# The output projection goes group by group; eight modulation matrices become rows between the gates

## The reference, cut to what matters

```
m   = silu(cond) @ mod_w + mod_b                      # 6 x 1024 values: sh1, sc1, g1, sh2, sc2, g2
h   = rms(x) * gain * (1 + sc1) + sh1
y   = mixer(h)                                        # layer 0: recurrent block, layer 1: pooling
x   = x + g1 * (rms(y) * gain)                        # the post norm
h   = rms(x) * gain * (1 + sc2) + sh2                 # the pre norm of the feed-forward part
x   = x + g2 * (rms(swiglu(h)) * gain)
```

```
gate, rec = split(h @ w_in);  u = conv4(rec)
a = exp(-8 * sigmoid(u @ wa + ba) * softplus(-lam));  b = sqrt(1 - a^2) * sigmoid(u @ wx + bx) * u
hf, hb = scan forward, scan backward of (a, b)
y = ((hf + hb) * gelu(gate)) @ w_out
```

## Time and profile before

| | |
|---|---|
| three runs, us | 2396.31, 2398.34, 2401.71 (median 2398.34) |
| profiled execution, us | 2397.51, span 2395.5 |
| busy, us (share of the span) | PE 2252.5 (94%), DVE 1378.0 (58%), POOL 974.1 (41%), ACT 840.7 (35%) |
| mean granted TensorE clock | 0.967 |
| w_lo of a weight on POOL (line 2186), 157 | 4.7 us each |
| w_hi of a weight on ACT (line 1194), 157 | 1.9 us each |
| load of a modulation matrix to raw, 42 | 5.1 us to landing |
| x_old from the stored residual, 1.5 MB | 7.4 us to landing |

### The profile page before, as it was taken

The page is one execution under the profiler, slowest core; times in us unless marked ns, Lnnn a source line. Parts: engine busy times, 40 slices in busy tenths (PEclk is TensorE's granted clock), DMA queues, the critical chain, the costliest instruction groups (busy, mean ns, idle before and its releaser), DMA issues.

```text
span 2395.5 us, 31600 instructions
## 1 busy us (share of the span) xinstructions
PE 2252.5 (94%) x12840; PEld 2215.0 (92%) x12840; DVE 1378.0 (58%) x2356; ACT 840.7 (35%) x1143; POOL 974.1 (41%) x380
## 2 busy tenths in 40 slices
PE   7888899896999999999999999899999999999996
PEld 4887899886999999999999999899999999999995
DVE  7679977856665566432466468558363232442344
ACT  3477763024311111222343455544352122111232
POOL 3433313444202210444562676575465265222441
PEclk8999999898999999999999999999999999999997
DMA  8211125343223333344232454353234233321322
GB/s 277 98 63 55 56 68 188 117 149 115 88 95 101 105 124 101 110 141 133 87 134 97 131 178 131 106 184 124 97 132 141 71 120 129 104 88 53 104 86 92
DMA packets 209616, 274.01 MB, mean 114 GB/s; under 512 B 4744, under 2 KB 192704, under 8 KB 208960
## 3 DMA queue, kind: packets, MB, share of 16 engines
q1 hardware_dynamic: 180544, 221.47, 28.1%
q10 hardware_dynamic: 27200, 41.09, 5.0%
q0 software_dynamic: 1728, 9.44, 1.0%
HBM read 243.66 MB, written 28.32 MB: 114 GB/s over the span
## 4 chain that ended last, share of the span: by engine, by line
PE 66%; DVE 10%; ACT 2%; issue 2%; POOL 1%; DMA 1%; ACTq 0%; DVEq 0%; POOLq 0%
PE bank L819 63%; DVE y L1748 3%; DVE y L1735 1%; DVE pool_sum L2091 1%; DVE mod_sum_norms L1665 1%; PE bank L867 1%; PE bank L898 1%; POOL w_lo L2186 1%; DVE hid_lo L2002 1%; DVE wide L1798 1%; DVE mv_lo L1785 1%; PE bank L887 1%; DVE wide L2113 0%; DMA raw<-in_l_ffn_w_in 0%; DVE mv_lo L2149 0%
## 5 line engine op out<-in xcount | busy, mean ns | idle before, releaser
L2186 POOL TENSOR_TENSOR w_lo<-raw,w_hi 128x2048 fp32r<-128x2048 f32 x157 | 735.1, 4695 | 1178.2 <-ACT w_hi L1194 1178.0
L819 PE MATMUL bank<-mv_hi,w_hi 128*128 128x384 f32 (+2 forms) x2736 | 931.5, 340 | 27.2 <-DVE mv_lo L1869 9.3
L819 PE MATMUL bank<-mv_lo,w_hi 128*128 128x384 f32 (+2 forms) x2736 | 923.5, 338 | 0.0
L819 PE MATMUL bank<-mv_hi,w_lo 128*128 128x384 f32 (+2 forms) x2736 | 923.0, 337 | 0.0
L819 PEld LDWEIGHTS bank<-mv_hi,w_hi 128*128 128x128 f32 x2736 | 519.2, 190 | 31.8 <-issue 25.5
L819 PEld LDWEIGHTS bank<-mv_lo,w_hi 128*128 128x128 f32 x2736 | 519.5, 190 | 0.0
L819 PEld LDWEIGHTS bank<-mv_hi,w_lo 128*128 128x128 f32 x2736 | 518.9, 190 | 0.0
L1194 ACT ACTIVATE w_hi<-raw 128x2048 fp32r<-128x2048 f32 x157 | 295.8, 1908 | 528.3 <-DMA raw<-in_l_ffn_w_out 216.1
L819 PE MATMUL bank<-hid_hi,w_hi 128*128 128x384 f32 (+2 forms) x1056 | 362.5, 343 | 19.7 <-DVE hid_lo L2002 19.5
L2020 DVE TENSOR_TENSOR y<-y,bank 128x384 f32<-128x384 f32 (+2 forms) x480 | 262.2, 554 | 202.1 <-PE bank L819 202.1
L1999 DVE TENSOR_TENSOR hid<-hid,bank 128x384 f32<-128x384 f32 (+2 forms) x132 | 72.9, 553 | 516.1 <-PE bank L819 513.9
(11 more groups left out here) (138 smaller groups left out, 1773.7 us busy)
## 6 DMA issues: line engine op xcount, KB each, us to landing
raw<-in_l_ffn_w_in SPq DMA_DIRECT2D x92, 1024.0 KB, 5.1
raw<-in_l_ffn_w_out SPq DMA_DIRECT2D x46, 1024.0 KB, 4.9
raw<-in_l_mod_w SPq DMA_DIRECT2D x42, 1024.0 KB, 5.1
residual<-y ACTq DMA_DIRECT2D x10, 1536.0 KB, 7.2
x_old<-residual ACTq DMA_DIRECT2D x10, 1536.0 KB, 7.4
raw<-in_l_w_in SPq DMA_DIRECT2D x8, 1024.0 KB, 5.4
mod_stage<-in_l_mod_w SPq DMA_DIRECT2D x6, 1024.0 KB, 12.9
recurrence<-lru_f POOLq DMA_DIRECT2D x8, 576.0 KB, 3.1
```

The source lines that it names most:

```text
L819: last = pe.matmul(out, w, x, start=start and n == 0, stop=stop and n == len(steps) - 1)
L2186: pool.tensor_tensor(w_lo[:, slot(w), :], raw[:, q % 2, :], w_hi[:, slot(w), :].bitcast(F32), ALU.subtract).then_inc(w_ready, 1)
```

## The change

1. Matrices 6 and 7 become rows like 0 to 5, and so do 8 to 15: one of them in each stage of the gates, product behind the gate units, turn behind the fills. ACT copies the row into `raw` and adds the bias. Matrices 16 to 19 stay sums.
2. In the gates `u_split_lo` and the lo parts of six weights (granules 4 to 9) move from POOL to VectorE.
3. The output projection goes group by group over all 8 tiles. Three weights fit, so weights 0 and 1 are loaded and split a second time for groups 1 and 2. ACT takes the result from PSUM, once squared, once as it is. VectorE makes the lo parts of the mixed rows of groups 1 and 2 and three of the weights' lo parts.
4. The norms of the mixer and their pre norms are planned and run beside the products, as in the later steps. The first feed-forward block is done for groups 0 and 1, then for group 2, with the same weights. `ffn_first` goes.

```diff
-STEPS = [together(range(NB - TURN)) + snake(list(range(NB - TURN, NB))),
+STEPS = [[(0, (0, 1)), (0, (2,))] + together(range(1, NB - TURN)) + snake(list(range(NB - TURN, NB))),
+WOUT_LOADS = (0, 1, 2, 3, 0, 1)
+WOUT_TURNS = ((0, 1, 2, 3), (1, 2, 3, 4), (2, 3, 4, 5))
-    order += MIX_PHASES[:-1] + mods(0, 8, 10) + MIX_PHASES[-1:]
-    order += [("w_out", 0)] + mods(0, 10, 12) + [("w_out", 1)] + mods(0, 12, 14) + [("w_out", 2)]
-    order += mods(0, 14, 20) + [("w_out", 3)]
+    for item in MIX_PHASES:
+        order.append(item)
+        order += mods(0, *MODS_BEHIND.get(item, (0, 0)))
+    order += [("w_out", 0)] + mods(0, 17, 18) + [("w_out", 1), ("w_out", 2), ("w_out", 3)] + mods(0, 18, 20)
+    order += [("w_out", 4), ("w_out", 5)]
...
-            units += gate_units(n, j) + FILLS[n, j]
+            m = FIRST_MODS + 2 * n + j
+            units += gate_units(n, j) + [("row", m, 0, 0)] + FILLS[n, j] + [("turn", m, 0, 0)]
...
+                if kind == "row":
+                    row_product(bank[P_BANK[p]][0:2, 0:2 * P], n).then_inc(p_ready, 1)
+                    return
+                if kind == "turn":
+                    pe.wait_ge(p_freed, UNIT["row", n, 0, 0] + 1)
...
+            def out_projection(g, upto):
+                for i in range(KT):
+                    n, w = O_WOUT + KT * g + i, WEIGHT["w_out", WOUT_TURNS[g][i // 2]]
+                    upto(AT_WOUT[n - O_WOUT])
...
+            def take_wout(g, i):
+                n, m = O_WOUT + KT * g + i, wout_tile(g, i)
+                if i == 0:
+                    act.wait_ge(*((acc_ready[g - 1], 2) if g else (mixed_ready, KT)))
+                act.wait_ge(out_ready, n + 1)
+                src = bank[OUT_BANK[n]][:, 0:GT]
+                act.activation(norm_squares_of(g, 1)[:, m], src, ACT.Square).then_inc(squares[g], 1)
+                squared[g] += 1
+                act.activation(group(y, g)[:, m], src, ACT.Copy).then_inc(wout_taken, 1)
...
             for n in range(NLB):
                 for j in range(2):
                     s = 4 * n + 2 * j
                     lru_input(s)
                     lru_input(s + 1)
                     if n < NLB - 1:
                         conv(n + 1, j)
+                    for w in NEXT_GRANULES["gates", (2 * n + j - 1) // 2, 1 - j] if s else []:
+                        split_lo(w)
+                    if j == 1 and n < NLB - 1:
+                        u_split_lo(n + 1, 0)
                     lru_step(s)
+                    if j == 1 and n < NLB - 1:
+                        u_split_lo(n + 1, 1)
                     lru_step(s + 1)
...
+            def first_norms(g):
+                yield
+                norm_begin(g)
+                yield from post_norm(g, 0, 1)
+                yield
+                norm_begin(g)
+                yield from pre_norm_split(g, 0, 2, 24)
```

More of the change, by code:

```diff
@@ L304, in product_times @@
     at, t, one = {}, 0.0, (GT + 32) / 2400
+    for n in W_OUTS:
+        t += 3 * KT * one
+        at["out", n] = t
     for what, n in PRODUCTS:
@@ L316 @@
 AT_PRODUCT = {"gate": 3 * KT * (GT + 32) / 2400, "out": 3 * HB * (GT + 32) / 2400}
+AT_WOUT = [AT["out", n] - AT_PRODUCT["gate"] for n in W_OUTS]
 def merged(times, chains):
@@ L343, with places @@
 ENDLESS = 1e9
+FIRST_END = 200.0
+PLACES = range(0, KT, 2)
+def places(t):
+    return [t + k / KT * AT_PRODUCT["gate"] for k in PLACES]
 def out_time(layer, g, m=KT - 1):
@@ L364, in feed_forward_work @@
     work, hooks = [], []
+    for i, n in enumerate(W_OUTS):
+        hooks += places(AT_WOUT[i])
+        work.append(("ACT", ("take", n), AT["out", n], TAKE))
+    for w, t in J1_SPLITS.items():
+        low = ("DVE", 2.2) if w in DVE_SPLITS else ("POOL", SPLIT_LO)
+        work += [("ACT", ("split", w), t, SPLIT_HI), (low[0], ("split", w), t + SPLIT_HI, low[1])]
+    for g, t in ((1, MIXED_T[0]), (2, MIXED_T[1])):
+        for part, (t0, t1) in enumerate(MIXED_PARTS):
+            work += [("ACT", ("mixed", g, part), t + part * 1e-3, 0.45 * (t1 - t0)),
+                     ("DVE", ("mixed", g, part), t + 0.5 + part * 1e-3, 0.5 * (t1 - t0))]
     for layer in range(2):
-        for s in range(1 - layer, len(STEPS[layer])):
+        for s in range(len(STEPS[layer])):
             groups = STEPS[layer][s][1]
             t = AT["gate", PAIR[layer, s, groups[0], 0]] - AT_PRODUCT["gate"]
-            w = WEIGHT["down", layer, s]
-            work += [("ACT", ("split", w), t, SPLIT_HI), ("POOL", ("split", w), t + SPLIT_HI, SPLIT_LO)]
+            if own(layer, s) == s:
+                w = WEIGHT["down", layer, s]
+                t += DOWN_LATER if (layer, s) == (0, 0) else 0.0
+                work += [("ACT", ("split", w), t, SPLIT_HI), ("POOL", ("split", w), t + SPLIT_HI, SPLIT_LO)]
             for g in groups:
@@ L446, in post, with first_norm, first_residual, first_split @@
         return ends
+    folded = [put(("PE", "mods", 0), 0.0, FOLD) for _ in range(2)]
+    for m in range(FIRST_SUM + 2, 20):
+        t = put(("DVE", "mods", 0), 0.0, MOD_SUM)
+        folded.append(put(("PE", "mods", 0), t, FOLD))
+    scale = put(("DVE", "mods", 0), folded[-1], 2 * SMALL)
+    chain = "first"
+    spread, landed = {}, {}
+    def first_norm(g):
+        squared = [due["ACT", "take", O_WOUT + KT * g + i] + TAKE for i in range(KT)]
+        landed[g] = put(("ACT", chain, g), squared[-1], 0.1) + LANDING
+        spread[g] = norm(chain, g, squared)
+    def first_residual(g):
+        ends = post(chain, g, max(landed[g], spread[g]))
+        sq = squares(chain, g, ends)
+        put(("ACT", chain, g), ends[-1], 0.1)
+        spread[g] = max(scale, norm(chain, g, sq))
+    def first_split(g):
+        hi = []
+        for k in range(KT):
+            t = put(("DVE", chain, g), spread[g], FIRST_DVE)
+            hi.append(put(("ACT", chain, g), t, OP["ACT"]))
+            if k >= SPLIT_LAG - 1:
+                t = put(("DVE", chain, g), hi[k - SPLIT_LAG + 1], FIRST_DVE)
+        for k in range(KT - SPLIT_LAG + 1, KT):
+            t = put(("DVE", chain, g), hi[k], FIRST_DVE)
+        s = next(s for s, (b, groups) in enumerate(STEPS[0]) if g in groups)
+        assert t < AT["gate", PAIR[0, s, g, 0]], (g, t, AT["gate", PAIR[0, s, g, 0]])
+    first_norm(0)
+    first_residual(0)
+    first_split(0)
+    first_norm(1)
+    first_residual(1)
+    first_norm(2)
+    first_split(1)
+    first_residual(2)
+    first_split(2)
     for g in range(NG):
@@ L989, in _ @@
                 kind, n, j, g = u[0], u[1], u[2], u[-1]
-                if (kind, n) not in seen:
+                if (kind, n) not in seen and kind not in ("row", "turn"):
                     seen.add((kind, n))
@@ L2342, in after_pairs @@
         first = PAIR[layer, s, STEPS[layer][s][1][0], 0]
-        if first:
-            places |= {first + i + lag: MOD["mod", *m] for i, m in enumerate(mods)}
+        places |= {first + i + lag: MOD["mod", *m] for i, m in enumerate(mods)}
     return places
```

599 lines of the change are left out of this document (322 added, 277 removed).

## The result

The kernel after takes 2370.7 us (median of 4 runs, 2367.4 to 2374.5), the kernel before 2397.3 (median of 4, 2389.7 to 2401.7): 26.6 us less, ratio 0.9887, 95% interval 0.9869 to 0.9905. Forecast were 2345 and a gain of 53.5, range 2326 to 2370. The profiled execution took 2369.3 us, its span is 2367.5.

What follows compares the result with a forecast made beforehand. Taken as bounds: VectorE at the start, VectorE with POOL in its way in the gates, a chain of small steps in the output projection. 9.5 + 3 + 3.2 + 37.8 = 53.5 us less gave 2345 us, range 2326 to 2370.

Steps and rivals of the forecast that it cites:

- Start: Up to the first product: matrices 6 and 7 as rows bring it from 70.87 to near 61.5, minus 9.5 us.
- eight rows of 3.6 and eight turns behind each other from 21.1 end at 52: Start: TensorE's row products and turns run back to back, ending at 52 us where the last turn ended at 61.6.
- The tail of 9.3: Start: coefficient, affine, hi and lo after the last turn, 9.3 us before the first product, taken as unchanged.
- Gates: Lo parts to VectorE, eight rows to TensorE: TensorE needs 206 us plus 3.6 idle, 209.7 in all, minus 3.
- Its chain becomes 39.6 - 8.1 - 11.5 = 20 us shorter, 193 us: Gates: VectorE regains 39.6 us lost to POOL and takes on 8.1 of u_lo and 11.5 of weight splits.
- 193 / 8: Gates: VectorE's chain of 193 us spread evenly over eight stages, 24.1 us each.
- two stages with three fills at 29.0 us: Gates: a stage with three fills asks 29.0 us of TensorE, one with a single fill 20.6.
- The rival of the turn behind ScalarE's copy: Gates: turn waits for ACT's copy behind tanh, exp and sqrt; 225 us, 12.4 above before, total 2360; chance 0.13.
- plus 31: Gates: upper bound, all of today's idle and slow time stays beside the new row work; lower bound minus 7.
- Rest of the input projection: Four folds of 0.8 us go where TensorE is full: minus 3.2 us.
- Output projection: With first feed-forward step: floor 199.8 us plus 13 of norm waits, 212.8 instead of 250.57, minus 37.8.
- Behind it: After 664.6 us order and work stay: the same 1731 us, within 3.

Runs made afterwards that it cites:

- Experiment 4: Kernel after with half of the tiles left out of each of the first eight row products: 2363.5 us, first product at 59.02.
- Experiment 2: Kernel before with only the gates' lo parts (u and weights 4 to 9) moved from GpSimd to VectorE, no rows there: 2398.8 us, ratio 1.0005.
- 11: Kernel after with ScalarE copying the row before Exp and Sqrt, full rows, and ScalarE's two Sqrt a stage left out: 2356.5 us.
- 6: Kernel after with ScalarE copying the row before Exp and Sqrt, and seven of eight products of each row among the gates left out: 2370.7 us.
- 10: Kernel after with the row copied before Exp, an eighth of each gate row's products, and ScalarE's two Sqrt a stage left out: 2354.5 us.
- all six kernels with these gates: The kernel after and five follow-up kernels whose gates have the same instructions; their gates took 219.6 to 223.7 us, mean 221.5.
- 8: Kernel after with rows, copies and turns of matrices 14 and 15, the two in the last pair of stages, left out: 2362.3 us.
- 5: Kernel after with ScalarE copying each gate row right behind the two Tanh instead of behind Exp and Sqrt: 2369.0 us.
- Experiment 12: Kernel after with GpSimd taking the mixer's first-group lo parts ahead of the lo part of w_out's second weight: 2363.6 us.
- 13: Kernel after with the lo parts of the output projection's fifth and sixth weight on VectorE instead of GpSimd: 2358.9 us.
- Experiment 3: Kernel after with the gates' lo parts back on GpSimd, the eight rows kept: 2367.0 us, gates 221.6.
- experiment 17: Kernel after with mixer lo parts ahead of the weight's on GpSimd, and the output projection's last two weights' lo parts on VectorE: 2354.4 us, ratio 0.9826.

## Why the prediction was wrong

**Start, 5.1 us short.** The failed step is "eight rows of 3.6 and eight turns behind each other from 21.1 end at 52". It left out the six norm steps that stand between them in TensorE's queue (0.83 and 0.93 us each, 5.3 together) and began 1.9 us early. The tail of 9.3 that I kept was 8.2, which took 1.1 of the miss back. Experiment 4 shows that this chain, and not a landing, was the bound.

**Gates, 14 us short, half of the miss.** The terms that could be read from rows were right: 128x1152 at 1.36 us, the split at 2.29 (2.3 forecast), TensorE's work 206 (207.9 measured), low idle. Counted on TensorE in the profiled execution, the 14 us are 6.0 more idle time than the 3.6 forecast, 6.2 of lower clock, nearly all of it behind the two turns, which the sum put at nothing, and 1.9 of work. What failed is the step before: "Its chain becomes 39.6 - 8.1 - 11.5 = 20 us shorter, 193 us", "against a VectorE chain of 193 / 8 = 24.1". It took VectorE's busy time, freed of GpSimd, for the length of a stage. Experiment 2 gives VectorE that time alone and gains nothing. In the kernel after no pair's length is one engine's sum alone. In the first three pairs three limits lie within a few us: TensorE's work with the rows, 54.0 and 58.3 us in the first and third (11); with nearly all of the rows taken out, still 54.9, 56.8 and 59.2 (6); and with ScalarE's block shortened as well, 52.5, 54.4 and 56.2 (10). Shortening any one, by 18 us of rows, 10 of convolution or 21 of Sqrt in the three, gave back 0 to 3 us a pair. Part of that is clock again: of the 56.8 and 59.2 us, 3.5 and 2.6 were lost to it. So these pairs did not become shorter by the change; they grew by 3.3 in the profiled execution. Of that 2.7 are the third pair, which took 59.3 or 59.4 us in all six kernels with these gates. This growth stood in the forecast's own figures: two stages with three fills at 29.0 us make 58.0 of TensorE's work in a pair that took 56.7, and only the sum over all stages hid it. The last pair is another case, which "193 / 8" hid: it has no convolution and VectorE is busy in it for only 30 us, so its two rows, the turns and the waits they bring count nearly in full. It grew by 7.7 us; 5.6 went with them (8), 4.0 with the early copy alone (5).

The rival of the turn behind ScalarE's copy (chance 0.13) was the mechanism of part of this: its two waits were there, with 2.8 us of lower clock behind each. Its size, 12.4 us above before for all stages, is near the 11.0 measured, but not for its reason: in the first three pairs the early copy freed no time. The bound "plus 31" covered the result; the value taken, near its lower end, was the error, argued from banks and not from what a stage waits for.

**Rest of the input projection:** 3.0 of 3.2, as forecast.

**Output projection, 8.6 us short.** The idle time was sized rightly: 14.7 us for norms and short step where 13 were forecast, 5.4 at the start for 6.2. The failed term is what comes behind a wait. From 1200 to 1800 the forecast took over the idle time alone, but the clock was 0.98 there, which over 600 us is some 12 us more. Here 12.7 us went in lower clock where 3.5 were set down. Experiment 12 took away the start's waits, 5.4 us less 2.2 new ones, and won 7.3: the lower clock went with them.

The rule of the Trainium skill (SBUF — State Buffer, Who interferes with whom) stands: VectorE with two SBUF inputs was held for as long as GpSimd's instruction ran, 4.58 us beside one of 4.63. The forecast weighed it with accumulations of 1 us and called the kernel's room wide enough. The instruction that holds is the longest one in GpSimd's queue, the weight split. Moving two of them to VectorE (13) gave 5.4 us in this stretch, second to the 7.3 of experiment 12; its total is the lowest of the single edits.

**Behind it:** -2.2 us, inside the 3 allowed, and less than the 9 us by which this code differs between executions.

**Open.** How the first three pairs' second limit is made up: round trip through ScalarE, VectorE's convolution and its scans each gave a part, none the whole. One link is plain in the trace of the kernel after: at 230.42 TensorE goes on 0.1 us after VectorE's second lo part of u, which stands in VectorE's order behind a scan, and that behind a wait of 1.55 us for ScalarE's Sqrt. Experiment 3, which moves it to GpSimd with the eleven others, waits 0.5 us or less there, and its third pair takes 58.3 us, TensorE's work alone; but its second is 0.8 us longer, with a turn waiting 4.76 us. 13's total gain (11.8 us) is over twice what its stretch shows (5.4): in its profiled execution 4.1 more stand in the gates and 2.1 behind, both inside what the same code differs by.

## What to carry to other kernels

Before pricing what a freed engine is worth, cut the stretch into its stages and ask of each which engine would wait less: where an engine already waits for another, as VectorE did for ScalarE, its savings turn into longer waits. A stage whose filler work is uneven, or whose last round lacks a part (no convolution), must be priced for itself. A wait of TensorE of a few us is to be booked with the lower clock behind it, and a long instruction of GpSimd that holds VectorE up belongs away from the short chain that everyone waits for. Where a queue waits for another engine's result only for the sake of its order, look at what stands behind that wait.

## What the runs showed of the hardware

- A wait of 2.92 us at the same instruction was followed by twelve gate products of 15.4 us in the kernel after, of 14.2 in experiment 17, and of 12.7, the time at the full clock, at one of the two places in experiments 12 and 13. So the lower clock came sooner, later or not at all in executions of the same code. No wait of 1.0 to 1.9 us before gate products was followed by it. Of the longer ones one of 2.06 us was and one of 2.40 was not (experiment 10), one of 3.75 was not (kernel before), and all of 3.79 us and more were, with 13.9 to 15.5 us for the twelve products. The gates of the same code differ by 4 us between executions, and this is most of it.
- ScalarE needs 9.8 us for a block of Tanh, Exp and Sqrt over 2 x 1152 columns, 2.6 of them for two table loads of 1.28.
- Moving 12 lo parts from GpSimd to VectorE, alone (experiment 2), took 18.3 us off VectorE's busy time (184.2 to 165.9) although it did 21.8 us of work more: running beside GpSimd's lo parts had been costing it 40 us, as the forecast read from the rows (39.6), and none of it was on the path.
